# A two-layer decoder trunk: expert weights in units of 1024, 1024, 1024 and 512 columns instead of four of 896, with six low-half buffers

## The chip, the core and the metric

The kernel runs on one core of a Trainium2 chip. Its time is that of one execution on the device in microseconds (us); lower is better. TensorE (PE) does the matrix products, and its weight loads run beside them (PEld); VectorE (DVE) and ScalarE (ACT) do the elementwise work, GpSimd (POOL) a little of it; SyncE (SP) issues the DMAs that bring the weights from HBM.

## The reference, cut to what matters

256 tokens of width 1024 go through two layers of token mixers, cross attention and a feed-forward part. In the first layer the latter is dense, in the second it has 8 experts, of which each token uses 2. All is in float32. The expert part, on which the change acts:

```python
D_MODEL, D_FF, N_EXPERTS, TOP_K = 1024, 3584, 8, 2
def swiglu(h, w_gu, w_down):
    g, u = jnp.split(h @ w_gu, 2, axis=-1)
    return (jax.nn.silu(g) * u) @ w_down
def moe_ffn(h, router_w, w_gu, w_down):
    ...
    for e in range(N_EXPERTS):
        out = out + gate[..., e:e + 1] * swiglu(h, w_gu[e], w_down[e])
    return out
```

## The kernel before

**Three products for one.** Every float32 weight block is landed by a DMA in one of six slots of `raw`. ACT copies it, rounded to the fast float32r type, to `w_hi`; DVE subtracts that from `raw` and so gets the low half. The activations are split likewise. PE then does three float32r products for one exact one: high by high, high by low, low by high (`expert_products`), each with its own 128x128 stationary operand.

**A job.** For each expert, up to 128 of its tokens are gathered by products with a 0/1 matrix (`gather`, two halves), multiplied by the gate (g), up (u) and down (d) weights, and scattered back by another product (`scatter`). The inner width of 3584 is cut in `XUNITS` = 4 units of `XW` = 896 columns. `JOB`, made by `plan_job`, lists the 48 blocks of weights of a job as (g, u or d; unit; piece). A gate or up block has 256 rows of 896 columns (896 KB) and takes 2 k-tiles x 2 halves x 3 = 12 matmuls of 448 columns. A down block has 256 rows of 1024 columns (1 MB, 12 matmuls of 512 columns), the fourth of each unit 128 rows (6 matmuls). The order is g0 u0, g1 u1 d0, g2 u2 d1, g3 u3 d2, d3. A loop runs job after job; this input takes eight of them.

**The pipeline.** Each engine goes through the blocks in the same order with its own program. At block o PE does its products and then what `expert_after` puts behind it; ACT and DVE do `expert_work` of block o, if it has any, and then the weight work of a later block: ACT the high half of block o + `LEAD` (5), DVE the low half of block o + `LOW_LEAD` (3). The low halves go round in `EXPERT_LO` = 4 buffers, each borrowed from a tile of the mixers that is idle by then. SP issues the load of block b when the low half of block b - 6 is done, since that frees the slot. Semaphores tell how far each engine is: `raw_landed`, `hi_done`, `lo_done`, `block_used`.

**Between the blocks.** When a unit's gate and up sums are complete, ACT takes silu (`x_silu`), DVE multiplies (`x_hid`), PE transposes `x_hid` in seven 128x128 tiles (`turn_expert`) behind the last gate block of the next unit, and ACT and DVE split the result into high and low (`expert_turned`, in the text: the turn). For unit 3 this happens behind block (d,2,1). The gather for the next job stands behind (d,3,0) and (d,3,1) on PE; ACT and DVE split what it brings (`gathered`), DVE ahead of the low halves that follow in its program. The first job also holds the arithmetic of the routing on DVE (`routing_left`).

The function below is what PE does for a block, its waits ahead of the products; the rest of the touched code follows it.

Of the kernel before, what the change touches and what calls it, by code (L numbers as in the profile page):

```python
# [27 lines left out]
ALU = mybir.AluOpType  # L28
# [3 lines left out]
P = 128  # L32
# [21 lines left out]
EXPERT_LO = 4  # L54
LOW_LEAD = 3
UNIT = 512
XUNITS = 4
XW = 896
# [56 lines left out]
def plan_job():  # L115

    order = [(w, 0, i) for w in "gu" for i in range(4)]
    for v in range(1, XUNITS):
        order += [(w, v, i) for w in "gu" for i in range(4)] + [("d", v - 1, i) for i in range(4)]
    return order + [("d", XUNITS - 1, i) for i in range(4)]  # L120
# [20 lines left out]
def build(nc, x_in, mem_in, positions, norm_mix, w_in, attn_sink, w_branch, w_out, pool_w, pool_scale,  # L141
# [19 lines left out]
    assert len(DENSE) == FFN_BLOCKS and XUNITS * XW == F and 2 * XW <= 4 * UNIT  # L161
# [6 lines left out]
    with ctx:  # L168
# [27 lines left out]
        area_a = sb("area_a", [P, 2048])  # L196
        area_b = sb("area_b", [P, 2048])
# [6 lines left out]
        decay = sb("decay", [P, 4, T])  # L204
        pool_m0 = sb("pool_m0", [P, 4, 144])
        pool_m1 = sb("pool_m1", [P, 4, P])
        mask_a = sb("mask_a", [P, T])
        mask_c = sb("mask_c", [P, T])
# [64 lines left out]

        x_hid = area_a[:, 0:XW]
        x_silu = area_b[:, 0:XW]
        feed_t = view(area_b, 0, KD, T)
        expert_lo_bufs = [expert_lo0, expert_lo1, expert_lo2, expert_lo3]
# [121 lines left out]
        def expert_width(b):  # L399
            which, v, i = JOB[b[1] % len(JOB)]  # L400
            return 2 * XW if which != "d" else (D if i == 3 else 2 * D)
# [65 lines left out]
        def expert_source(e, o):  # L467
            which, v, i = JOB[o]
            if which == "d":
                rows = 2 * P if i < 3 else P  # L470
                return moe_w_down[0, bass.ds(e, 1), v * XW + i * 2 * P:v * XW + i * 2 * P + rows, :].rearrange(
                    "a (k p) n -> p (a k) n", p=P)
            col = v * XW + "gu".index(which) * F
            return moe_w_gu[0, bass.ds(e, 1), i * 2 * P:(i + 1) * 2 * P, col:col + XW].rearrange(
                "a (k p) n -> p (a k) n", p=P)
# [38 lines left out]
        def expert_hid_t(part, v):  # L514
            return stat1[:, part, 0:7, (v % 2) * P:(v % 2) * P + P]
# [14 lines left out]
        def _(sp):  # L530
# [8 lines left out]
            def load_expert(e, o, base, after_use=False):  # L539
# [6 lines left out]
                sp.dma_start(expert_raw(b).rearrange("p (k n) -> p k n", n=XW if JOB[o][0] != "d" else D),  # L546
# [166 lines left out]
        def _(act):  # L713
# [342 lines left out]
            def expert_work(j, o, first):  # L1056
# [3 lines left out]
                if which == "g" and i == 3:  # L1060
# [3 lines left out]
                    act.activation(x_silu[:, 0:448], bank[0][:, 0:448], ACT.Silu)  # L1064
                    act.activation(x_silu[:, 448:896], bank[1][:, 0:448], ACT.Silu).then_inc(ffn_silu.sem, 1)
# [11 lines left out]
                elif (which, v, i) == ("d", XUNITS - 1, 3):  # L1077
# [4 lines left out]
            def expert_turned(turn, v):  # L1082

                act.wait_ge(ffn_tr.sem, ffn_tr.at(turn, "tr"))
                act.activation(expert_hid_t(0, v)[:, 0:4, :], bank[4][:, :].rearrange("p (k n) -> p k n", k=4), ACT.Copy)
                act.activation(expert_hid_t(0, v)[:, 4:7, :], bank[5][:, 0:3 * P].rearrange("p (k n) -> p k n", k=3),  # L1086
                               ACT.Copy).then_inc(ffn_hi.sem, 1)
# [59 lines left out]
        def _(dve):  # L1147
# [495 lines left out]
            def expert_work(j, o, first):  # L1643
# [3 lines left out]
                if which == "u" and i == 3:  # L1647
# [4 lines left out]
                    dve.tensor_tensor(x_hid[:, 0:448], bank[2][:, 0:448], x_silu[:, 0:448], ALU.mult)  # L1652
                    dve.tensor_tensor(x_hid[:, 448:896], bank[3][:, 0:448], x_silu[:, 448:896], ALU.mult).then_inc(ffn_hid.sem, 1)
                elif which == "g" and i == 3 and v:
# [16 lines left out]
            def expert_turned(turn, v):  # L1671

                dve.wait_ge(ffn_hi.sem, ffn_hi.at(turn, "hi"))
                dve.tensor_tensor(expert_hid_t(1, v)[:, 0:4, :], bank[4][:, :].rearrange("p (k n) -> p k n", k=4),  # L1674
                                  f32_of(expert_hid_t(0, v)[:, 0:4, :]), ALU.subtract)
# [741 lines left out]
```

## Time and profile before

| | |
|---|---|
| Time, median of 3 runs | 2102.28 us (2102.07 to 2103.97) |
| The profiled execution | 2105.14 us, of which the span is 2103.4 us |
| Busy in the span | PE 2063.5, PEld 1771.3, DVE 1516.9, ACT 1273.9, POOL 56.0 us |
| HBM | 523.88 MB read, 250 GB/s over the span |
| TensorE clock granted | 0.993 of full speed on average |

The profiled execution is 2.86 us above the median of the runs; a difference worked out from its trace is set off from the median as it stands. A busy share sums over stages: a page of the profile gives it in 40 slices of 52.6 us, and the expert part fills the last 20.

### The profile page before, as it was taken

What the parts mean: (1) busy time and instruction counts of PE and PEld (TensorE: products, weight loads), DVE (VectorE), ACT (ScalarE), POOL (GpSimd) and SP (SyncE); (2) the same over time, 40 slices, a digit from 0 to 9 for tenths busy, and PEclk for the clock granted to TensorE, in tenths of its full rate; (3) what the DMA queues carried; (4) which work ended last, traced back from release to release, by engine and by line L of the source; (5) the groups of instructions that cost most, each with busy time, mean ns of one, the idle gap of its engine ahead of it and who ended that gap; (6) DMA issues with size and microseconds to landing.
All of it is one profiled execution on the core that took longest, in us unless ns stands there. A gap on an engine that the chain in (4) does not pass through costs nothing.

```text
span 2103.4 us, 26982 instructions
## 1 busy us (share of the span) xinstructions
PE 2063.5 (98%) x10103; PEld 1771.3 (84%) x10103; DVE 1516.9 (72%) x1498; ACT 1273.9 (61%) x1312; POOL 56.0 (3%) x134
## 2 busy tenths in 40 slices
PE   7999999999999999999989999999999999999997
PEld 6788888888888888888878888888888888888886
DVE  5776565555556776564379788888888888888897
ACT  6466545454344466545466766777666777767676
POOL 3300000000000300000000000000000000000000
PEclk9999999999999999999989999999999999999999
DMA  7444554455555444554469999899999999999994
GB/s 252 160 141 140 172 188 161 140 181 189 191 189 180 162 144 138 179 180 160 141 227 359 333 349 358 317 377 331 341 344 334 363 331 349 337 348 368 325 356 166
DMA packets 191708, 526.00 MB, mean 250 GB/s; under 512 B 10440, under 2 KB 17680, under 8 KB 191632
## 3 DMA queue, kind: packets, MB, share of 16 engines
q1 hardware_dynamic: 191632, 524.96, 70.4%
q8 instruction: 51, 0.84, 0.2%
q14 instruction: 25, 0.20, 0.0%
HBM read 523.88 MB, written 1.05 MB: 250 GB/s over the span
## 4 chain that ended last, share of the span: by engine, by line
PE 90%; DVE 5%; issue 2%; ACT 2%; SPq 1%; DMA 0%; POOL 0%; DVEq 0%; ACTq 0%
PE bank L1871 13%; PE bank L2269 13%; PE bank L1873 13%; PE bank L1872 13%; PE bank L2271 13%; PE bank L2270 13%; DVE expert_lo L1170 3%; PE bank L1904 2%; PE bank L2339 2%; PE bank L2349 1%; PE bank L2331 1%; PE bank L1940 1%; PE bank L1921 1%; PE bank L2019 1%; PE bank L2038 1%
## 5 line engine op out<-in xcount | busy, mean ns | idle before, releaser
L724 ACT ACTIVATE w_hi<-raw 128x1792 fp32r<-128x1792 f32 (+2 forms) x389 | 655.0, 1708 | 223.0 <-DMA raw<-in_moe_w_gu 179.2
L1170 DVE TENSOR_TENSOR expert_lo<-raw,w_hi 128x1792 fp32r<-128x1792 f32 (+2 forms) x387 | 758.4, 2017 | 0.9 <-ACT w_hi L724 0.7
L2269 PE MATMUL bank<-w_hi,stat 128*128 128x448 f32 (+1 forms) x1472 | 561.7, 382 | 8.0 <-DVE expert_lo L1170 7.9
L2271 PE MATMUL bank<-w_hi,stat 128*128 128x448 f32 (+1 forms) x1472 | 548.7, 373 | 0.0
L2270 PE MATMUL bank<-expert_lo,stat 128*128 128x448 f32 (+1 forms) x1472 | 548.5, 373 | 0.0
L1871 PE MATMUL bank<-w_hi,stat 128*128 128x512 f32 (+1 forms) x1296 | 512.1, 395 | 4.7 <-DVE low_in_place L1151 4.7
L1873 PE MATMUL bank<-w_hi,stat 128*128 128x512 f32 (+1 forms) x1296 | 504.4, 389 | 0.0
L1872 PE MATMUL bank<-low_in_place,stat 128*128 128x512 f32 (+1 forms) x1296 | 503.7, 389 | 0.0
L1151 DVE TENSOR_TENSOR low_in_place<-raw,w_hi 128x2048 fp32r<-128x2048 f32 (+1 forms) x162 | 368.8, 2281 | 185.5 <-ACT w_hi L718 185.1
L718 ACT ACTIVATE w_hi<-raw 128x2048 fp32r<-128x2048 f32 (+1 forms) x162 | 306.9, 1904 | 163.1 <-DMA raw<-in_dense_w_gu 57.2
L2269 PEld LDWEIGHTS bank<-w_hi,stat 128*128 128x128 f32 x1472 | 276.5, 188 | 51.5 <-DVE expert_lo L1170 15.5
L2270 PEld LDWEIGHTS bank<-expert_lo,stat 128*128 128x128 f32 x1472 | 276.8, 188 | 33.8 <-issue 3.3
L2271 PEld LDWEIGHTS bank<-w_hi,stat 128*128 128x128 f32 x1472 | 276.4, 188 | 33.4
L1871 PEld LDWEIGHTS bank<-w_hi,stat 128*128 128x128 f32 x1296 | 244.5, 189 | 55.4 <-issue 7.0
L1873 PEld LDWEIGHTS bank<-w_hi,stat 128*128 128x128 f32 x1296 | 244.3, 188 | 50.7
L1872 PEld LDWEIGHTS bank<-low_in_place,stat 128*128 128x128 f32 x1296 | 244.5, 189 | 47.7
L1674 DVE TENSOR_TENSOR stat<-bank,stat 128x512 fp32r<-128x512 f32 x32 | 22.1, 692 | 94.4 <-ACT stat L1086 94.4
L1093 ACT ACTIVATE stat<-bank,gains 128x128 fp32r<-128x128 f32 x72 | 20.5, 368 | 51.1 <-PE bank L2339 51.1
L1705 DVE SCALAR_TENSOR_TENSOR stat<-bank,gains,stat 128x128 fp32r<-128x128 f32 x72 | 20.3, 344 | 38.4 <-ACT stat L1093 38.4
L792 ACT ACTIVATE gate<-bank,rs_mix 128x512 f32<-128x512 f32 x16 | 11.0, 688 | 50.0 <-PE bank L1873 49.9
L2339 PEld LDWEIGHTS bank<-heads_t,tok 128*128 128x128 f32 x288 | 37.6, 205 | 2.3 <-issue 1.0
L1684 DVE TENSOR_TENSOR x<-x,bank 128x512 f32<-128x512 f32 x32 | 20.5, 684 | 25.9 <-PE bank L2349 25.9
(269 smaller groups left out, 1233.7 us busy)
## 6 DMA issues: line engine op xcount, KB each, us to landing
raw<-in_moe_w_gu SPq DMA_DIRECT2D x256, 896.0 KB, 7.0
raw<-in_moe_w_down SPq DMA_DIRECT2D x96, 1024.0 KB, 8.0
raw<-in_w_in SPq DMA_DIRECT2D x56, 1024.0 KB, 5.0
raw<-in_dense_w_gu SPq DMA_DIRECT2D x28, 1024.0 KB, 5.1
raw<-in_w_branch SPq DMA_DIRECT2D x16, 1024.0 KB, 5.0
raw<-in_w_xkv SPq DMA_DIRECT2D x16, 1024.0 KB, 5.1
raw<-in_moe_w_down SPq DMA_DIRECT2D x32, 512.0 KB, 7.8
raw<-in_dense_w_down SPq DMA_DIRECT2D x14, 1024.0 KB, 5.1
```

What stands on the lines that cost most here:

```text
L718: act.activation(w_hi[:, slot(b), :, 0:width], raw[:, slot(b), :, 0:width], ACT.Copy).then_inc(hi_done, 1)
L724: act.activation(expert_hi(b), expert_raw(b), ACT.Copy).then_inc(hi_done, 1)
L1151: dve.tensor_tensor(in_place_lo(b)[:, :, 0:width], raw[:, slot(b), :, 0:width], f32_of(w_hi[:, slot(b), :, 0:width]), ALU.subtract).then_i ...
L1170: dve.tensor_tensor(expert_low(b), expert_raw(b), f32_of(expert_hi(b)), ALU.subtract).then_inc(lo_done, 1)
L1871: pe.matmul(dst, x_hi, wh, start=start, stop=False)
L1872: pe.matmul(dst, x_hi, wl, start=False, stop=False)
L1873: return pe.matmul(dst, x_lo, wh, start=False, stop=stop)
L1904: ins = pe.transpose(b[:, i * P:(i + 1) * P], src, ident[:, :])
L2269: pe.matmul(dst[:, 0:n], x_hi, wh[:, at], start=start, stop=False)
L2270: pe.matmul(dst[:, 0:n], x_hi, wl[:, at], start=False, stop=False)
L2271: ins = pe.matmul(dst[:, 0:n], x_lo, wh[:, at], start=False, stop=stop)
L2339: ins = pe.matmul(bank[4 + i][:, k * P:(k + 1) * P], tok[:, t, kt * P:(kt + 1) * P], pick[:, t, :], start=(t == 0), stop=(t == NT - 1))
```

## The change

The inner width is cut in units of 1024, 1024, 1024 and 512 columns. Every block is now 1 MB (256 rows x 1024, or 512 rows x 512 for gate and up of unit 3), every block has 12 matmuls and every product of a block is 512 columns wide. A unit of 1024 has 4 pieces each of g, u and d, the unit of 512 has 2: 42 blocks a job. The matmuls of a job's blocks go from 384 of 448 columns and 168 of 512 to 504 of 512; the transposes stay 28. The low halves get six buffers, two more taken from tiles of the mixers (`area`, `shapes`), and are made one block further ahead (`LOW_LEAD` 4). The gather's first half stands behind (d,2,3), ahead of all of d3, with a wait for the split of unit 3's turned tiles (`ffn_lo`), whose banks it overwrites; its second half stands behind (d,3,0).

```diff
-EXPERT_LO = 4
-LOW_LEAD = 3
+EXPERT_LO = 6
+LOW_LEAD = 4
-XW = 896
+XW = [1024, 1024, 1024, 512]
...
+def pieces(v):
+    return XW[v] // 256
...
-        area_a = sb("area_a", [P, 2048])
-        area_b = sb("area_b", [P, 2048])
+        area, area_low = sb_shared("area", [P, 4096], "area_low", [P, 4096])
+        area_a, area_b = area[:, 0:2048], area[:, 2048:4096]
+        expert_lo4 = area_low[:, 1024:3072]
...
+        shapes, expert_lo5 = sb_shared("shapes", [P, 2112], "expert_lo5", [P, 2112])
...
-        expert_lo_bufs = [expert_lo0, expert_lo1, expert_lo2, expert_lo3]
+        expert_lo_bufs = [expert_lo0, expert_lo1, expert_lo3, expert_lo2, expert_lo4, expert_lo5]
...
+            rows = D // pieces(v)
+            return moe_w_gu[0, bass.ds(e, 1), i * rows:(i + 1) * rows, col:col + XW[v]].rearrange(
...
                 elif (which, v, i) == ("d", XUNITS - 1, 1):
                     gathered(j + 1, 1)
-                elif (which, v, i) == ("d", XUNITS - 1, 3):
                     act.wait_ge(block_used, used_at((job_base(j), o)))
                     act.activation(y_sb[:, 0:512], bank[6][:, :], ACT.Copy)
...
-                        at = slice((k * len(dsts) + h) * n, (k * len(dsts) + h) * n + n)
+                        at = slice((k * len(dsts) + h) * 512, (k * len(dsts) + h) * 512 + 512)
-                        pe.matmul(dst[:, 0:n], x_hi, wh[:, at], start=start, stop=False)
+                        pe.matmul(dst[:, :], x_hi, wh[:, at], start=start, stop=False)
...
-                    expert_products(b, [bank[two], bank[two + 1]], stat0, 2 * i, slice(0, P), 2, XW // 2, i == 0, i == 3)
+                    two, ktiles = 2 * "gu".index(which), KD // pieces(v)
+                    expert_products(b, [bank[two + h] for h in range(XW[v] // 512)], stat0, ktiles * i, slice(0, P),
+                                    ktiles, i == 0, last_piece(v, i))
...
                 elif (which, v, i) == ("d", XUNITS - 2, 1):
-                    turn_expert(turn + 1)
-                elif (which, v, i) == ("d", XUNITS - 1, 0):
+                    turn_expert(turn + 1, v + 1)
+                elif (which, v, i) == ("d", XUNITS - 2, 3):
+                    pe.wait_ge(ffn_lo.sem, ffn_lo.at(turn + 1, "lo"))
                     pe.wait_ge(pick_ready.sem, pick_ready.at(j + 1, "pick"))
                     gather(0)
-                elif (which, v, i) == ("d", XUNITS - 1, 1):
+                elif (which, v, i) == ("d", XUNITS - 1, 0):
                     gather(1)
```

DVE's program from the turn of unit 3 to the end of a job, before. The low buffer's number is the block's place modulo 4; the first row pair is the turn, the `stat0` rows are `gathered`.

```order
L1674 TENSOR_TENSOR stat1<-bank4,stat1 128x4x128
L1676 TENSOR_TENSOR stat1<-bank5,stat1 128x3x128
L1170 TENSOR_TENSOR expert_lo0<-raw,w_hi 128x2048
L1170 TENSOR_TENSOR expert_lo1<-raw,w_hi 128x2048
L1170 TENSOR_TENSOR expert_lo2<-raw,w_hi 128x2048
L1705 SCALAR_TENSOR_TENSOR stat0<-bank4,gains,stat0 128x128 x4
L1170 TENSOR_TENSOR expert_lo3<-raw,w_hi 128x1024
L1705 SCALAR_TENSOR_TENSOR stat0<-bank5,gains,stat0 128x128 x4
L1170 TENSOR_TENSOR expert_lo0<-raw,w_hi 128x1792
L1170 TENSOR_TENSOR expert_lo1<-raw,w_hi 128x1792
L1170 TENSOR_TENSOR expert_lo2<-raw,w_hi 128x1792
```

The row behind the turn is the low half of (d,3,0), and the first 128x1792 row, behind both `gathered`, that of (g,0,0) of the next job. The same stretch of DVE's program in the changed kernel, where `area_low` is the buffer of (d,3,0), `expert_lo5` that of (d,3,1) and `expert_lo0` that of the next (g,0,0):

```order
L1663 TENSOR_TENSOR area<-bank2,area 128x512
L1180 TENSOR_TENSOR expert_lo2<-raw,w_hi 128x2048
L1180 TENSOR_TENSOR area_low<-raw,w_hi 128x2048
L1688 TENSOR_TENSOR stat1<-bank4,stat1 128x4x128
L1180 TENSOR_TENSOR expert_lo5<-raw,w_hi 128x2048
L1180 TENSOR_TENSOR expert_lo0<-raw,w_hi 128x2048
L1180 TENSOR_TENSOR expert_lo1<-raw,w_hi 128x2048
L1718 SCALAR_TENSOR_TENSOR stat0<-bank4,gains,stat0 128x128 x4
L1180 TENSOR_TENSOR expert_lo3<-raw,w_hi 128x2048
L1718 SCALAR_TENSOR_TENSOR stat0<-bank5,gains,stat0 128x128 x4
L1180 TENSOR_TENSOR expert_lo2<-raw,w_hi 128x2048
```

The low half of (d,3,0) now stands ahead of the turn and that of the next (g,0,0) ahead of both `gathered`; the turn of unit 3 has one instruction for two. On PE, the first half of the gather stood before between the last product of (d,3,0) and the first of (d,3,1):

```order
L2269 MATMUL bank7<-w_hi,stat1 128x512
L2270 MATMUL bank7<-expert_lo0,stat1 128x512
L2271 MATMUL bank7<-w_hi,stat1 128x512
L2339 MATMUL bank4<-heads_t,tok 128x128 x8
L2269 MATMUL bank6<-w_hi,stat1 128x512
L2270 MATMUL bank6<-expert_lo1,stat1 128x512
```

Now it stands between the last product of (d,2,3), whose low buffer is `expert_lo2`, and the first of (d,3,0):

```order
L2282 MATMUL bank7<-w_hi,stat1 128x512
L2283 MATMUL bank7<-expert_lo2,stat1 128x512
L2284 MATMUL bank7<-w_hi,stat1 128x512
L2354 MATMUL bank4<-heads_t,tok 128x128 x8
L2282 MATMUL bank6<-w_hi,stat1 128x512
L2283 MATMUL bank6<-area_low,stat1 128x512
```

The gather moved up by one block. Between its second half and the next job's first block stands now (d,3,1), where (d,3,2) and the half block (d,3,3) stood before.

## Rows read from the trace of the kernel before

**Rows 1.** The page, by engine: busy us (share of the span) x instructions

```profile
PE 2063.5 (98%) x10103; PEld 1771.3 (84%) x10103; DVE 1516.9 (72%) x1498; ACT 1273.9 (61%) x1312; POOL 56.0 (3%) x134
```

**Rows 2.** The chain that ended last: start us, us, what

```profile
1183.34 1.78 PE bank L2339 x16
...
2077.70 1.78 PE bank L2339 x16
```

**Rows 3.** Groups by line and shape: shapes, count, busy us, mean ns, idle before

```profile
L1170 DVE TENSOR_TENSOR expert_lo<-raw,w_hi 128x1792 fp32r<-128x1792 f32 x259 | 508.8, 2017 | 0.9 <-ACT w_hi L724 0.7
...
L2269 PE MATMUL bank<-w_hi,stat 128*128 128x448 f32 x1024 | 383.4, 374 | 4.9 <-DVE expert_lo L1170 4.9
...
L1170 DVE TENSOR_TENSOR expert_lo<-raw,w_hi 128x2048 fp32r<-128x2048 f32 x96 | 215.9, 2282 | 0.0
L724 ACT ACTIVATE w_hi<-raw 128x2048 fp32r<-128x2048 f32 x96 | 181.7, 1928 | 37.0 <-DMA raw<-in_moe_w_down 36.9
...
L1170 DVE TENSOR_TENSOR expert_lo<-raw,w_hi 128x1024 fp32r<-128x1024 f32 x32 | 38.9, 1216 | 0.0
```

**Rows 4.** Waits on PE, from 1064 to 1112 us, then from there on

```profile
PE bank L2269 <- DVE expert_lo L1170: 2.7, 4, 1.0
...
PE bank L2269 <- DVE expert_lo L1170: 5.2, 16, 0.6
```

**Rows 5.** Timeline of PE, blocks without a wait: start us, us, instruction

```profile
1866.87 0.36 PE L2270 MATMUL bank<-expert_lo,stat 128*128 128x448 f32 x1
...
1876.39 0.40 PE L2269 MATMUL bank<-w_hi,stat 128*128 128x512 f32 x1
...
1881.62 0.39 PE L2271 MATMUL bank<-w_hi,stat 128*128 128x512 f32 x1
```

**Rows 6.** Timeline of PE at the end of a job

```profile
1813.96 0.93 PE L2331 MATMUL bank<-ident,area_a 128*128 128x128 f32 x7
...
1818.60 0.39 PE L2271 MATMUL bank<-w_hi,stat 128*128 128x512 f32 x1
1819.35 0.50 PE L2269 MATMUL bank<-w_hi,stat 128*128 128x512 f32 x1 [0.37 <-DVE expert_lo L1170]
1819.69 0.39 PE L2270 MATMUL bank<-expert_lo,stat 128*128 128x512 f32 x1
...
1832.38 0.39 PE L2271 MATMUL bank<-w_hi,stat 128*128 128x512 f32 x1
1833.00 0.47 PE L2269 MATMUL bank<-w_hi,stat 128*128 128x448 f32 x1 [0.23 <-DVE expert_lo L1170]
```

**Rows 7.** Timeline of DVE over the same stretch

```profile
1816.55 0.55 DVE L1676 TENSOR_TENSOR stat<-bank,stat 128x384 fp32r<-128x384 f32 x1
1817.02 6.68 DVE L1170 TENSOR_TENSOR expert_lo<-raw,w_hi 128x2048 fp32r<-128x2048 f32 x3
...
1829.89 1.13 DVE L1705 SCALAR_TENSOR_TENSOR stat<-bank,gains,stat 128x128 fp32r<-128x128 f32 x4 [2.26 <-ACT stat L1093]
1830.93 3.95 DVE L1170 TENSOR_TENSOR expert_lo<-raw,w_hi 128x1792 fp32r<-128x1792 f32 x2
```

**Rows 8.** Timeline of DVE at the routing and in the first job

```profile
1052.14 2.02 DVE L1170 TENSOR_TENSOR expert_lo<-raw,w_hi 128x1792 fp32r<-128x1792 f32 x1
...
1092.06 2.03 DVE L1170 TENSOR_TENSOR expert_lo<-raw,w_hi 128x1792 fp32r<-128x1792 f32 x1
...
1095.82 2.02 DVE L1170 TENSOR_TENSOR expert_lo<-raw,w_hi 128x1792 fp32r<-128x1792 f32 x1
```

**Rows 9.** DMA, 1370 to 1970 us: GB/s in 40 slices; queue: packets, MB, share; issues

```profile
GB/s 398 340 384 360 337 273 373 296 361 363 351 382 355 272 376 326 320 380 347 380 344 317 292 378 308 358 376 352 385 357 257 376 322 317 382 345 397 352 335 275
...
q1 hardware_dynamic: 58921, 206.98, 93.9%
...
raw<-in_moe_w_gu SPq DMA_DIRECT2D x150, 896.0 KB, 7.0
```

**Rows 10.** DMA in the dense part, 440 to 640 us, the queue's row

```profile
q1 hardware_dynamic: 19515, 37.59, 56.5%
```

More of the change, by code:

```diff
@@ L160, in build @@
     LAYER_BLOCKS = MIX_BLOCKS + FFN_BLOCKS
[L161 removed]
+    assert len(DENSE) == FFN_BLOCKS and sum(XW) == F and 2 * max(XW) <= 4 * UNIT
     assert len(JOB) % CYCLE == 0 and len(JOB) % EXPERT_LO == 0
@@ L1059, in expert_work @@
                 turn = j * XUNITS + v
-                if which == "g" and i == 3:
+                if which == "g" and last_piece(v, i):
                     act.wait_ge(block_used, used_at((job_base(j), o)))
@@ L1063, in expert_work @@
                         act.wait_ge(ffn_hid.sem, ffn_hid.at(turn - 1, "hid"))
-                    act.activation(x_silu[:, 0:448], bank[0][:, 0:448], ACT.Silu)
-                    act.activation(x_silu[:, 448:896], bank[1][:, 0:448], ACT.Silu).then_inc(ffn_silu.sem, 1)
+                    for h in range(XW[v] // 512):
+                        ins = act.activation(x_silu[:, h * 512:(h + 1) * 512], bank[h][:, :], ACT.Silu)
+                    ins.then_inc(ffn_silu.sem, 1)
                     if v:
@@ L1646, in expert_work @@
                 turn = j * XUNITS + v
-                if which == "u" and i == 3:
+                if which == "u" and last_piece(v, i):
                     dve.wait_ge(ffn_silu.sem, ffn_silu.at(turn, "silu"))
@@ L1651, in expert_work @@
                         dve.wait_ge(ffn_tr.sem, ffn_tr.at(turn - 1, "tr"))
[L1652 to L1654 removed]
+                    for h in range(XW[v] // 512):
+                        ins = dve.tensor_tensor(x_hid[:, h * 512:(h + 1) * 512], bank[2 + h][:, :],
+                                                x_silu[:, h * 512:(h + 1) * 512], ALU.mult)
+                    ins.then_inc(ffn_hid.sem, 1)
+                elif which == "g" and v and last_piece(v, i):
                     expert_turned(turn - 1, v - 1)
@@ L2259, in dense_unit_block, with expert_products @@
                     feed_rows(0, 1)
-            def expert_products(b, dsts, stationary, k0, cols, ktiles, n, first, last):
+            def expert_products(b, dsts, stationary, k0, cols, ktiles, first, last):
                 wh, wl = expert_hi(b), expert_low(b)
@@ L2307, in expert_after @@
                     scatter(j - 1, 1, 4)
-                elif which == "g" and i == 3 and v:
+                elif which == "g" and v and last_piece(v, i):
                     if v == 1 and not first:
```

63 lines of the change are left out of this document (31 added, 32 removed).

## The prediction, made before the changed kernel was run

> **What bounds the kernel now.** I read the page first. PE is busy 98% of the span [rows 1], at a clock that was granted to 0.993, so the question is not whether PE is fed but what spaces its instructions. The chain that ended last comes by the same gather once a job; over seven jobs (1183.34 to 2077.70) that is 894.36 us, 127.8 us a job [rows 2]. The waits by releaser say what PE lacks: in the first job it sits idle four times for 2.7 us, in the rest of the expert part 16 times for 5.2 us, each time for a low half from DVE [rows 4]. So PE's own spacing is the bound, and the waits are two small ones at the end of each job. The bound next to it is DMA: in 600 us of steady jobs its queue was busy 93.9% of the time [rows 9]. That is close enough to have to be priced. DVE is third; its low halves take, a job, 32 x 1.965 + 12 x 2.249 + 4 x 1.216 = 94.7 us of the 127.8, from busy time by count [rows 3].
>
> **Term 1, wider products.** The columns that pass through PE stay the same (384 x 448 = 336 x 512); 48 matmuls a job are saved, and with them what one costs beyond its columns. The timeline of PE gives the spacing. From 1866.87 to 1876.39 there are 47 steps of 448 columns, over three block borders: 202.6 ns each. From 1876.39 to 1881.62 there are 23 steps of 512: 227.4 ns [rows 5]. So a job's gate and up blocks take 384 x 0.2026 = 77.8 us now and 336 x 0.2274 = 76.4 us then: 1.4 us less, 11.2 over eight jobs. Two digits in the starts leave 0.2 us a job either way, 9.6 to 12.8. The border between blocks costs PE nothing (the 47 steps cross three), so fewer blocks save nothing more.
>
> The 64 more columns cost 24.8 ns; at that rate 448 columns are 174 ns, and 29 ns of each step are the price that 48 matmuls a job no longer pay. The Trainium skill ("TensorE: Matmul & The Clock Gate", section "Wait — 56ns, not 53.3ns?") gives columns by 2.4 GHz plus about 2.5 ns as the spacing; by it 48 matmuls less save 0.12 us a job, 1.0 in all, and the sum below would end 10 us higher. The rows are of this kernel's pairs of load and product, and I go by them.
>
> **Term 2, the wait at (d,3,0).** PE starts the last product of (d,2,3) at 1818.60 and the next at 1819.35, 0.52 us later than its spacing allows, and the one behind it comes 0.34 on, 0.11 late [rows 6]. On DVE the low half of (d,3,0) starts at 1817.02, right behind the turn of unit 3; it is the first of three in 6.68 us, so it takes about 2.25 and ends at 1819.3 [rows 7]. In the changed program this low half stands ahead of the turn, where DVE has time. What is late next is the turn's low part itself, for which PE now waits ahead of the gather, with the whole PE program queued behind it. It was done at 1817.10, PE's last product of (d,2,3) at 1818.8: 1.7 us to spare, and the turn of unit 3 now has one instruction for two on ACT and on DVE (0.55 less there). I take the wait as gone: 0.63 x 8 = 5.0 us.
>
> **Term 3, the wait at (g,0,0).** From 1832.38 to 1833.00 PE loses 0.39 us, and about 0.11 with the restart as above. DVE's low half starts at 1830.93, behind the `gathered` of 1829.89 [rows 6, 7]. Now it stands ahead of both. (g,0,0) then needs `gathered` of the first half: PE has (d,3,0), the second gather and (d,3,1) in between, 2 x 2.73 + 1.8 = 7.3 us, for a split of 1.13 us on DVE [rows 7] behind a like one on ACT. The second half is first used by (g,0,2), three blocks or 8.2 us behind its gather. Gone too: 0.50 x 7 = 3.5 us, since the last job has no next.
>
> **Term 4, the first job.** DVE does one step of the routing between each two of its low halves, which start 3.76 us apart (1092.06, 1095.82) [rows 8], while PE takes a block in 12 x 0.2026 = 2.43. PE waits four times, 2.7 us in idle time [rows 4]; with the restarts (0.63 lost for 0.37 shown above) that is about 3.8. Then a low half takes 2.25, so the distance is 4.0, a block 2.73; the loss per step stays 1.3. But one more block of low halves is ready, which is worth 2.7: 1.1 stays, 2.7 is won. Against it, the low half at 1052.14 stands ahead of the routing with nothing to hide it, and grows by 0.25 to 0.3. Net 2.4 us, between 0 (if DVE uses up the lead before) and 3.8.
>
> **Term 5, stray waits.** Of the 5.2 us, 8 x 0.37 + 7 x 0.23 = 4.6 are the two regular ones; 0.6 shown, some 1.0 lost, belong to one more. One block more of lead covers it: 1.0 (0 to 1).
>
> **What costs nothing.** DVE's low halves become 42 x 2.249 = 94.5 us a job, as now. Unit 3 is short, so less stands between things: the turn of unit 2 comes behind its last gate block, and only (u,3,0) and (u,3,1) are left ahead of (d,2,0). From the start of the transposes to DVE's end of the turn the trace shows 1813.96 to 1817.10, 3.1 us [rows 6, 7]; PE needs 0.9 for the transposes and 5.5 for the two blocks to get to (d,2,0). That is 3 us to spare, behind which the whole of d2 would stand. The copy of the job's output by ACT moves with the job's last block and keeps what follows it.
>
> **DMA, the cover that has to hold.** A job loads 42 x 1.0486 = 44.0 MB. The terms make it 127.65 - 1.4 - 0.63 - 0.50 = 125.1 us, so the mean rate goes from 345 to 352 GB/s. At a share of 93.9% the queue moved 206.98 MB in 600 us [rows 9]; a share of 100% at the same time per packet would be 367 GB/s, or 120.0 us a job. PE stays the bound by 5 us a job. While blocks follow each other without anything between, PE asks for 1.0486 MB in 2.73 us, 384 GB/s (377 now), and slices of 15 us show up to 398 [rows 9]. The loop of a slot also closes: 7.0 us to land for 896 KB [rows 9], so 8.0 for 1 MB, 1.9 and 2.25 for the halves [rows 3], 12.2 in all against six blocks or 16.4 us. The Trainium skill ("DMA: Bandwidth & Descriptors", section Specifications) gives about 358 GB/s as HBM's limit for a core. The slices above it disagree; and by it a job could not be shorter than 123.0 us, which still leaves PE the bound.
>
> **The sum.** 11.2 + 5.0 + 3.5 + 2.4 + 1.0 = 23.1 us off the profiled execution's 2105.14: 2082.0. The median of the runs is 2.86 lower, so off it: 2079.2, say 2079.5. With all terms at their low ends and the regular waits gone: 9.6 + 8.5 = 18.1, 2084.2; at their high ends 12.8 + 8.5 + 3.8 + 1.0 = 26.1, 2076.2. The likeliest case's own range is 2076 to 2085. A measurement of this kernel can tell a change from none at about 0.2%, 4.2 us.
>
> **The rivals.**
> - *Only the waits go.* The spacing of 512 was read on down blocks, whose stationary operand comes from another tile than that of gate and up. If the price of a matmul beyond its columns is not saved there, or the regular waits come back in another place, 5 to 11 us are missing: 2085 to 2092. By the page's rule on spacing, worked as rows (48 x 2.5 ns in place of 1.4 us a job), it would be 2089.7. Against it: the operand has the same shape and type in both. 0.14.
> - *DMA holds the pace.* If 93.9% is as full as the queue gets, a job stays at 127.65 us and only the first job's gain is left: 2098 to 2103. For it: ACT waits for transfers, 36.9 us for the down blocks alone [rows 3]. Against it: DVE hardly ever waits for them (0.7 us [rows 3]) and the slices at 398. 0.08.
> - *Slower: the new shapes of the gate and up transfers are dearer.* The dense part's rows of 2 KB moved 37.59 MB in 200 us at a share of 56.5% [rows 10]: 333 GB/s when full. If all transfers went like that, a job would take 132.2 us, 4.6 more than now: 2102 + 8 x 4.6 = 2139. It decides from where the full rate falls below 345. For it: 4 of 42 blocks do get rows of 2 KB. Against it: the other 38 have rows of 4 KB, longer than now; with 4 blocks at 333 and 38 at 367 the job needs 121.2 us. 0.05.
> - *More than forecast*, below 2076: the spacing at its better end and no wait left anywhere. 0.06.
> - *A new wait in the short unit*, some 1 us a job or more, in place of those removed: 0.05, about 2086 to 2095.
>
> The forecast keeps 0.62.
>
> **How the numbers follow.** 2079.5 is the likeliest case. From 2074 to 2094 lie the forecast, the first and the last rival and most of the fourth; left out are DMA's two, 0.13, and the rest of the fourth, 0.04. Faster by over 0.2% (below 2098): 0.88. Within: 0.06, nearly all DMA holding the pace. Slower: 0.06.
>
> **What would show it right or wrong.** The changed trace should show the spacing of gate and up products at 227.4 ns; 48 matmuls less per job; no idle time ahead of (d,3,0) and (g,0,0); gathers 125.1 us apart; DMA at 352 GB/s and a share near 95% or less; in the first job one or two waits of a microsecond together. If the gathers are 127 us apart with DVE waiting for ACT and ACT for DMA, the second rival is right. If the spacing in unit 3, where twelve products in a row go to one bank, or in the gate and up blocks is above 230 ns, term 1 fails.

## The result and the profile of the changed kernel

| | before | changed |
|---|---|---|
| Median | 2103.12 us (2102.07 to 2104.83, 4 runs) | 2076.7 us (2076.33 to 2077.05, 4 runs) |
| Ratio, 95% interval | | 0.9873 (0.9859 to 0.9886) |
| Profiled execution, its span | 2105.14, 2103.4 us | 2076.53, 2074.8 us |

The change makes the kernel 26.4 us faster, 1.3%. The page by engine, busy us (share) x instructions, answers to [rows 1], and its costliest groups to [rows 3]:

```profile
PE 2042.9 (98%) x9719; PEld 1699.7 (82%) x9719; DVE 1516.0 (73%) x1435; ACT 1258.4 (61%) x1248; POOL 56.0 (3%) x134
...
PE 96%; DVE 1%; ACT 1%; SPq 1%; issue 1%; DMA 0%; POOL 0%; DVEq 0%; ACTq 0%
...
L733 ACT ACTIVATE w_hi<-raw 128x2048 fp32r<-128x2048 f32 x341 | 636.2, 1921 | 105.7 <-PE bank L2284 65.0
...
L2282 PE MATMUL bank<-w_hi,stat 128*128 128x512 f32 x1344 | 534.5, 398 | 0.3 <-DVE stat L1718 0.3
```

The row of the page of before that goes with the last of these, both widths together:

```profile
L2269 PE MATMUL bank<-w_hi,stat 128*128 128x448 f32 (+1 forms) x1472 | 561.7, 382 | 8.0 <-DVE expert_lo L1170 7.9
```

384 matmuls are gone (8 x 48). The second line is the share of each engine in the chain that ended last: nearly all of it is PE (90% before, with 5% of DVE). The idle time ahead of L2282 is 0.3 us where L2269 had 8.0. ACT, which waited for transfers, now waits most for PE to give a `w_hi` buffer back (65.0 us): the engines ahead of PE run into its heels.

The chain of waits gives the pace, as in [rows 2]; L2354 is the gather, two rows a job:

```profile
1176.67 1.78 PE bank L2354 x16
1181.19 1.78 PE bank L2354 x16
...
2050.68 1.78 PE bank L2354 x16
2055.20 1.78 PE bank L2354 x16
```

From the first to the third row shown are seven jobs: 874.01 us, 124.86 each, against 127.8. In what follows a job is counted from its first gate product to the next job's. Before, six jobs behind the first took 127.45 to 128.35, 127.78 on average; the same jobs now take 124.86 each, all alike within 0.02. The waits of PE over the whole rest of the expert part, 1112 to 2076 us, in answer to [rows 4] (line and releaser: us, times, longest):

```profile
PE bank L2364 <- issue: 1.2, 1, 1.2
```

That is one pause in the tail, ahead of the last scatter; the 16 waits for low halves are gone. Around the gather, in answer to [rows 6], PE goes

```profile
1800.58 0.39 PE L2284 MATMUL bank<-w_hi,stat 128*128 128x512 f32 x1
1800.80 1.95 PE L2354 MATMUL bank<-heads_t,tok 128*128 128x128 f32 x16
1802.51 0.48 PE L2282 MATMUL bank<-w_hi,stat 128*128 128x512 f32 x1
1802.82 0.40 PE L2283 MATMUL bank<-area_low,stat 128*128 128x512 f32 x1
```

without a bracket, and DVE, in answer to [rows 7]:

```profile
1793.67 2.29 DVE L1180 TENSOR_TENSOR area_low<-raw,w_hi 128x2048 fp32r<-128x2048 f32 x1
1796.14 0.69 DVE L1688 TENSOR_TENSOR stat<-bank,stat 128x512 fp32r<-128x512 f32 x1 [0.19 <-ACT stat L1095]
...
1803.96 1.13 DVE L1718 SCALAR_TENSOR_TENSOR stat<-bank,gains,stat 128x128 fp32r<-128x128 f32 x4 [0.53 <-ACT stat L1103]
```

The low half of (d,3,0), `area_low`, is done at 1795.96; PE wants it at 1802.8. DVE's brackets, here 0.19 and 0.53, are its own spare time. DMA between 1370 and 1970 us, in answer to [rows 9]:

```profile
GB/s 411 335 403 362 338 310 321 346 402 326 400 357 365 321 317 332 380 354 379 378 369 341 318 287 376 408 340 382 346 361 319 330 330 395 335 400 365 348 318 324
...
q1 hardware_dynamic: 60098, 211.96, 94.6%
...
raw<-in_moe_w_gu SPq DMA_DIRECT2D x132, 1024.0 KB, 7.0
```

353 GB/s on average and landings in 7.0 us, as long as those of 896 KB before.

**Where the 28.6 us between the two spans lie.** The first expert product starts at 1065.80 before and at 1064.05 after; the first job takes 128.16 and 121.5; six more jobs give 6 x 2.92 = 17.5; from the start of the last job to the end it is 142.8 and 140.1. In all 1.75 + 6.66 + 17.5 + 2.7. The 1.75 is no work of the change. In windows (the granted TensorE clock is the third value from the end) the part ahead of the experts differs in one place, before and after:

```profile
60.00:80.00 20.00, 18.53 (x84) 14.88 (x83) 16.68 (x33) 6.00 (x7) 8.20 (x4) 0.91 0.47 156
```

```profile
60.00:80.00 20.00, 18.56 (x93) 14.97 (x93) 17.04 (x35) 6.18 (x8) 8.21 (x4) 1.00 0.48 158
```

In the profiled execution of the kernel before, the granted clock fell to 0.5, its 1.2 GHz level, for 3.4 us from 68.7 on, right behind a 1.47 us wait of PE for `gate`; after an equal wait in the other trace it did not. Up to there the starts of PE's matmuls in the two traces differ by 0.1 us at most, and from there to the experts by 1.7. That execution was 2.0 us above the median of the four runs, and so the medians differ by 26.4 and not by 28.6.

### The profile page after: what moved, and what is told of

It reads as the page before. It is cut to its first block, busy times and chain, and to the rows that moved or that the text cites. A ratio compares the mean times of both kernels' runs of the same rounds, so it can differ in the third digit from the quotient of the medians.

```text
span 2074.8 us, 26022 instructions
## 1 busy us (share of the span) xinstructions
PE 2042.9 (98%) x9719; PEld 1699.7 (82%) x9719; DVE 1516.0 (73%) x1435; ACT 1258.4 (61%) x1248; POOL 56.0 (3%) x134
## 4 chain that ended last, share of the span: by engine, by line
PE 96%; DVE 1%; ACT 1%; SPq 1%; issue 1%; DMA 0%; POOL 0%; DVEq 0%; ACTq 0%
PE bank L2282 15%; PE bank L2284 15%; PE bank L2283 15%; PE bank L1884 14%; PE bank L1886 13%; PE bank L1885 13%; PE bank L1917 2%; PE bank L2354 2%; PE bank L2364 1%; PE bank L2346 1%; PE bank L1953 1%; PE bank L1934 1%; PE bank L2032 1%; PE bank L2051 1%; SPq L541 1%
## 5 line engine op out<-in xcount | busy, mean ns | idle before, releaser
L733 ACT ACTIVATE w_hi<-raw 128x2048 fp32r<-128x2048 f32 x341 | 636.2, 1921 | 105.7 <-PE bank L2284 65.0
L1180 DVE TENSOR_TENSOR expert_lo<-raw,w_hi 128x2048 fp32r<-128x2048 f32 x284 | 637.3, 2287 | 0.2
L2282 PE MATMUL bank<-w_hi,stat 128*128 128x512 f32 x1344 | 534.5, 398 | 0.3 <-DVE stat L1718 0.3
L2284 PE MATMUL bank<-w_hi,stat 128*128 128x512 f32 x1344 | 524.2, 390 | 0.0
L1161 DVE TENSOR_TENSOR low_in_place<-raw,w_hi 128x2048 fp32r<-128x2048 f32 (+1 forms) x162 | 368.8, 2281 | 187.0 <-ACT w_hi L727 186.7
L2283 PE MATMUL bank<-expert_lo,stat 128*128 128x512 f32 x1120 | 436.2, 389 | 0.0
L2282 PEld LDWEIGHTS bank<-w_hi,stat 128*128 128x128 f32 x1344 | 252.5, 188 | 54.0 <-issue 3.4
L2284 PEld LDWEIGHTS bank<-w_hi,stat 128*128 128x128 f32 x1344 | 252.3, 188 | 53.3
L1884 PEld LDWEIGHTS bank<-w_hi,stat 128*128 128x128 f32 x1296 | 244.1, 188 | 55.3 <-issue 7.0
L1886 PEld LDWEIGHTS bank<-w_hi,stat 128*128 128x128 f32 x1296 | 243.9, 188 | 50.6
L2283 PEld LDWEIGHTS bank<-expert_lo,stat 128*128 128x128 f32 x1120 | 210.5, 188 | 45.4 <-issue 3.3
L1180 DVE TENSOR_TENSOR area_low<-raw,w_hi 128x2048 fp32r<-128x2048 f32 x56 | 128.2, 2289 | 8.1 <-ACT w_hi L733 8.1
L2283 PE MATMUL bank<-area_low,stat 128*128 128x512 f32 x224 | 87.2, 389 | 0.0
L2283 PEld LDWEIGHTS bank<-area_low,stat 128*128 128x128 f32 x224 | 42.1, 188 | 8.3
L1095 ACT ACTIVATE stat<-bank 128x512 fp32r<-128x512 f32 x56 | 31.0, 606 | 26.2 <-PE bank L2346 26.2
```

The costliest lines, as they stand in the source:

```text
L733: act.activation(expert_hi(b), expert_raw(b), ACT.Copy).then_inc(hi_done, 1)
L1161: dve.tensor_tensor(in_place_lo(b)[:, :, 0:width], raw[:, slot(b), :, 0:width], f32_of(w_hi[:, slot(b), :, 0:width]), ALU.subtract).then_i ...
L1180: dve.tensor_tensor(expert_low(b), expert_raw(b), f32_of(expert_hi(b)), ALU.subtract).then_inc(lo_done, 1)
L1884: pe.matmul(dst, x_hi, wh, start=start, stop=False)
L1886: return pe.matmul(dst, x_lo, wh, start=False, stop=stop)
L2282: pe.matmul(dst[:, :], x_hi, wh[:, at], start=start, stop=False)
```

## The experiments

**Theory**: the gain has three parts that add up. Wider products save PE some 1.4 to 1.7 us a job; the regular waits at (d,3,0) and (g,0,0) go because of the longer lead; the lead covers the routing in the first job. **Rival 1**: the regular waits have another cause that the new units or the gather's place take away by themselves, and the lead does nothing in a steady job. **Rival 2**: the products save less, and what looks like it is fewer waits.

**One part undone, or one done alone.** Three kernels start from the changed one. `a_width_only` keeps only the new units and the six buffers:

```diff
-LOW_LEAD = 4
+LOW_LEAD = 3
...
-                elif (which, v, i) == ("d", XUNITS - 2, 3):
-                    pe.wait_ge(ffn_lo.sem, ffn_lo.at(turn + 1, "lo"))
+                elif (which, v, i) == ("d", XUNITS - 1, 0):
...
-                elif (which, v, i) == ("d", XUNITS - 1, 0):
+                elif (which, v, i) == ("d", XUNITS - 1, 1):
```

`a_lead3` has the first hunk of this alone, `a_gather_late` the other two alone. Two start from the kernel before, with its four units of 896: `b_lead4` takes the six buffers, with the tiles that are lent for them, and the lead,

```diff
-EXPERT_LO = 4
-LOW_LEAD = 3
+EXPERT_LO = 6
+LOW_LEAD = 4
```

and `b_gather_up` the move of the gather alone (the hunks above in reverse).

Expected of `a_width_only`: 

> The changed kernel with the low halves three blocks ahead again and the gather behind (d,3,0) and (d,3,1) again, so that the new units and the six buffers are what is left of the change. Theory 1 (the prediction's own: the lead takes away the two regular waits): PE waits again at (d,3,0) and (g,0,0), 1.13 us a job, jobs 126.0 us apart, the waits of the first job are back with some 4 us and the stray ones with 1 to 2; about 2090. Theory 2 (the short last unit alone takes them away, since its turn is shorter and the next job's first low half then stands ahead of both splits of the gather): jobs stay within 0.2 us of 124.86, only the first job and stray waits cost, 4 to 6 us; about 2082.

Expected of `a_lead3`: 

> The changed kernel with the low halves three blocks ahead in place of four. Theory 1: the low half of (d,3,0) is behind the turn again, but the gather now stands ahead of that block and hides it; jobs at 124.9 us, first job and stray waits back, 4 to 6 us: 2081 to 2083. Theory 2 says the same number, and that a_width_only is no slower than this one. If the lead were worth the regular waits here too, it would be 2089 or more.

Expected of `a_gather_late`: 

> The changed kernel with the gather behind (d,3,0) and (d,3,1) again, four blocks of lead kept. Theories 1 and 2: no wait comes back, 2077, jobs at 124.9 us. Rival (the gather had to move because the unit of 512 leaves too few blocks behind it): PE waits at (g,0,0) or (g,0,2) for the split of the gathered rows, 0.5 to 2 us a job, 2081 to 2092.

Expected of `b_lead4`: 

> The kernel before, units of 896 and its own gather, with six low buffers and four blocks of lead. Theories 1 and 2: the waits at (d,3,0) and (g,0,0) go, jobs from 127.45 (the best of before) to 126.3 us; first job and stray waits go too, 4 and 2 us: 8.5 + 6 = 14 us less than before, about 2089. Rival (the waits move to something else in the same place, such as the split of the turn): less than 5 us gained, 2098 or more. If it gets below 2086, the spacing of the products is worth less than the 12 us I gave it.

Expected of `b_gather_up`: 

> The kernel before with the gather moved up by one block (behind (d,2,3) and (d,3,0), with the wait for the turn's low part ahead of it) and nothing else. Theory 2 (each part of the change removes the regular waits by itself, so their 8.5 us must not be counted once for each part): the waits at (d,3,0) and (g,0,0) go, jobs 126.5 us apart as in b_lead4, but the waits of the first job and the stray ones stay: 8 to 9 us below before. Theory 1 (only the lead takes them away): no more than 2 us below before.

| kernel | median us | ratio to before, 95% | first job | steady job |
|---|---|---|---|---|
| before | 2103.12 | | 128.16 | 127.45 to 128.35 |
| `b_gather_up` | 2094.16 | 0.9958 (0.9944 to 0.9973) | 127.70 | 126.48 |
| `b_lead4` | 2091.13 | 0.9935 (0.9918 to 0.9952) | 124.76 | 126.48 |
| `a_width_only` | 2081.97 | 0.9893 (0.9876 to 0.9909) | 123.86 | 124.86 |
| `a_lead3` | 2079.7 | 0.9881 (0.9864 to 0.9897) | 124.85 | 124.86 |
| `a_gather_late` | 2079.42 | 0.9885 (0.9868 to 0.9901) | 121.41 | 124.86 |
| changed | 2076.7 | 0.9873 (0.9859 to 0.9886) | 121.50 | 124.86 |

Each ratio is to the kernel before as measured together with that kernel, whose median was 2103.12 for the changed kernel, 2104.62 for `b_gather_up` and 2104.8 for the other four. The job lengths are from one trace each; the steady value is that of at least five of the six jobs, and the sixth is 0.14 us longer in `b_gather_up` and 0.05 in `a_width_only`.

The last column decides. There are two values for a steady job without waits: 126.48 with units of 896 and 124.86 with the new ones. Each part alone reaches the value of its units. The lead alone removes both regular waits, the gather's move alone removes both, and the new units alone do. Rival 1 holds in this form: the two waits had a margin so thin that any of the three edits covered it. The stray waits of the steady jobs go with them, in `b_gather_up` too, which has neither the lead nor the buffers (it keeps the 0.14 us). The six buffers were not run alone; before, DVE waited 0.9 us in all ahead of its low halves of 128x1792, 0.7 of it for ACT [rows 3], so hardly ever for a buffer. Rival 2 falls: with no wait on either side the new units are worth 126.48 - 124.86 = 1.62 us a job.

Beside the expectations: `a_width_only` came to 2081.97 where the second theory said about 2082 and the first about 2090, and `b_gather_up` to 10.5 us below its own before, where the second said 8 to 9 and the first at most 2. `a_lead3` came out 1.3 us under its range, `b_lead4` 2.1 us over its number (two waits of the first job stayed) and `a_gather_late` 2.4 us over, for a reason that neither theory had and that follows below.

The first job is where the lead still pays. PE's waits in `a_lead3` and, for comparison, in `b_lead4` (start, us, instruction, idle time before it):

```profile
1095.08 0.50 PE L2282 MATMUL bank<-w_hi,stat 128*128 128x512 f32 x1 [0.69 <-DVE expert_lo L1180]
1099.22 0.47 PE L2282 MATMUL bank<-w_hi,stat 128*128 128x512 f32 x1 [0.19 <-DVE expert_lo L1180]
1103.16 0.50 PE L2282 MATMUL bank<-w_hi,stat 128*128 128x512 f32 x1 [0.97 <-DVE expert_lo L1180]
1106.56 0.50 PE L2282 MATMUL bank<-w_hi,stat 128*128 128x512 f32 x1 [0.38 <-DVE expert_lo L1180]
```

```profile
1099.75 0.47 PE L2270 MATMUL bank<-w_hi,stat 128*128 128x448 f32 x1 [0.26 <-DVE expert_lo L1171]
1102.75 0.47 PE L2270 MATMUL bank<-w_hi,stat 128*128 128x448 f32 x1 [0.29 <-DVE expert_lo L1171]
```

With the new units, lead 3 leaves the four waits that the kernel before had, and 124.85 - 121.50 = 3.35 us is what lead 4 takes off. `a_width_only` has three such waits and a first job 1.0 us shorter than `a_lead3`, though PE's program is the same up to them; why one wait is missing was not followed up.

The gather's move shows only at the very end. The tail of `a_gather_late`'s chain, then of the changed kernel's:

```profile
2057.57 1.80 PE bank L2353 x16
2059.91 0.64 ACT stat L1103 x2
2061.09 0.61 DVE stat L1718 x2
2061.75 5.41 PE bank L2363 x8
```

```profile
2055.20 1.78 PE bank L2354 x16
...
2059.72 1.22 issue
2060.95 3.69 PE bank L2364 x8
```

At the old place the second gather stands next to the end, for a job that does not exist, and its split by ACT and DVE comes ahead of the last scatter: from the start of the last job to the end it takes 143.0 us and not 140.1. Of these 3.0 us, 1.25 are the later start of the last scatter. The other 1.7 are its length, 5.41 for 3.69: behind PE's wait of 2.4 us ahead of it the granted clock fell to 0.5, the 1.2 GHz level, from 2061.8 on for 3.4 us, and in the changed kernel it stayed at 1.0 there. `a_width_only` has the same wait, the same fall and the same 143.0. The last two kernels of the table differ by 2.7 us in the medians; steady jobs are alike. The kernel before had two more down pieces behind its second gather, which hid this. So with the new units alone the tail would have grown, and the move of the gather keeps it from that.

**The price of a matmul beyond its columns.** In the prediction this was 29 ns, a line through 448 and 512 columns. Four kernels take fewer columns in the block products of the changed one, so that a part of every product is left out (half, a quarter, an eighth, a sixteenth); loads, weights and everything else stay:

```diff
+                n = 384
...
-                        pe.matmul(dst[:, :], x_hi, wh[:, at], start=start, stop=False)
+                        pe.matmul(dst[:, 0:n], x_hi, wh[:, at], start=start, stop=False)
```

Expected with 384: 

> The changed kernel with 384 of the 512 columns in every product of a block; a quarter of each product is left out, all loads and splits stay. Linear theory (0.3875 ns a column and 29 ns a matmul, as the two widths of before give): spacing 178 ns. Floor theory (a matmul takes the longer of its columns and its weight load of 188 ns, and 14 ns more): 202 ns as with 448 columns. Page's rule (columns by 2.4 GHz and 2.5 ns): 162 ns. In each of these PE would need at most 112 us a job, so another engine sets the pace: DMA at 120.0 us a job by my estimate of 367 GB/s at a full share, 123.0 by the 358 GB/s of the page, below 115 if neither holds. VectorE has 110 us of work a job.

Expected with 256: 

> The same with 256 of the 512 columns; half of each product is left out. Linear theory: spacing 128 ns. Floor theory: 202 ns still. The job as in c_cols384 if DMA or VectorE is the bound there, since their work is the same.

Expected with 448: 

> 448 of the 512 columns in every product of a block (an eighth of each product is left out). With 256, 384 and 512 columns the spacing was 120.0, 173.6 and 227.2 ns, a line of 0.42 ns a column and about 13.5 ns beside it; at 448 that line gives 200.4 ns. If the 202.8 ns of the kernel before belongs to the width of 448, it shows up here again: 202.8 ns, and a job of 504 x 0.2028 + some 10.3 us of the rest = 112.5 us. If it belonged to the layout of the blocks before (rows of 896 columns in the weight operand), the spacing here is 200.4 ns and a job 111.3 us.

Expected with 480: 

> 480 of the 512 columns (a sixteenth of each product is left out). The line through 256, 384 and 512 gives 213.8 ns. If a width that is no multiple of 128 costs some 2.5 ns more in itself, it is 216.3 ns; if only 448 does, 213.8.

They ran once each and took 1955.76 (256), 1957.26 (384), 1985.79 (448) and 2035.44 us (480); what is read from them is the spacing in their traces. The first and the last start of 72 products in a row with 384, 448 and 480 columns, and with 512 in the changed kernel; between them are 71 steps:

```profile
1825.39 0.42 PE L2283 MATMUL bank<-w_hi,stat 128*128 128x384 f32 x1
...
1837.78 0.33 PE L2285 MATMUL bank<-w_hi,stat 128*128 128x384 f32 x1
```

```profile
1889.34 0.45 PE L2283 MATMUL bank<-w_hi,stat 128*128 128x448 f32 x1
...
1903.80 0.36 PE L2285 MATMUL bank<-w_hi,stat 128*128 128x448 f32 x1
```

```profile
1950.20 0.46 PE L2283 MATMUL bank<-w_hi,stat 128*128 128x480 f32 x1
...
1965.67 0.38 PE L2285 MATMUL bank<-w_hi,stat 128*128 128x480 f32 x1
```

```profile
1971.67 0.47 PE L2282 MATMUL bank<-w_hi,stat 128*128 128x512 f32 x1
...
1987.89 0.39 PE L2284 MATMUL bank<-w_hi,stat 128*128 128x512 f32 x1
```

The first step of a row holds some 0.08 us of the transposes ahead of it. Over the rows of the whole expert part without it and without waits the spacing is 173.6, 202.7, 216.7 and 227.1 ns; with 256 columns, where PE waits for DVE ahead of most blocks, it is about 120 ns within a block, here 20 steps in 2.40 us at a granted clock of 1.0:

```profile
1611.42 0.28 PE L2283 MATMUL bank<-w_hi,stat 128*128 128x256 f32 x1
...
1613.82 0.28 PE L2285 MATMUL bank<-w_hi,stat 128*128 128x256 f32 x1
```

None of the three spacings expected for 384 columns (178, 202 and 162 ns) came out. For 448 and 480 it is the theory in which the width itself costs more, 202.8 and 216.3 ns. Beside columns at 2.4 GHz (106.7, 160.0, 186.7, 200.0, 213.3 ns) there remain

| columns | 256 | 384 | 448 | 480 | 512 |
|---|---|---|---|---|---|
| ns beyond the columns | 13 | 13.6 | 16.0 | 16.7 | 13.8 |

There is a price of some 13.5 ns at every width, and the two widths that are no multiple of 128 cost some 2.5 to 3 ns more; whether it is this that they have in common, two widths do not show. It belongs to the width and not to the layout of the weights before: rows of 448 columns taken out of blocks of 512 show it too. So the 1.6 us a job have two sources: 48 matmuls less, 48 x 13.6 = 0.65 us, and 384 matmuls at an awkward width, 384 x 2.4 = 0.92 us; 1.57 together. A weight load is busy for 188 ns in every one of these kernels and yet products start 120 ns apart: it is no floor. The Trainium skill ("TensorE: Matmul & The Clock Gate", section "Wait — 56ns, not 53.3ns?") has 2.5 ns beyond the columns; these pairs of load and float32r product measure 13.5.

The same runs show what DMA can give. For 384 columns, 1300 to 1900 us: the queue, ACT's group and one of DVE's, then the window (behind its length the busy time of PE, PEld, DVE, ACT and POOL):

```profile
q1 hardware_dynamic: 68935, 244.36, 102.8%
```

```profile
L733 ACT ACTIVATE w_hi<-raw 128x2048 fp32r<-128x2048 f32 x234 | 446.7, 1925 | 105.0 <-DMA raw<-in_moe_w_gu 81.2 <-DMA raw<-in_moe_w_down 19.6 <-PE bank L2285 3.8
...
L1688 DVE TENSOR_TENSOR stat<-bank,stat 128x512 fp32r<-128x512 f32 x39 | 25.2, 683 | 9.1 <-ACT stat L1095 9.1
```

```profile
1300.00:1900.00 600.00, 564.12 (x3185) 531.07 (x3184) 590.95 (x400) 495.28 (x368) 0.00 (x0) 0.99 1.03 407
```

407 GB/s at a share of 102.8%, with ACT waiting for transfers and the steady jobs of both the 256 and the 384 column kernel at 107.7 to 109.1 us, 108.2 on average. The rate is the job's 44.04 MB by its length, so it is a rate that can be had and no proof that DMA is the bound there. DVE is busy 590.95 of the 600 us, 106.6 a job, and its idle time stands ahead of the turn's low part (9.1 us, 1.6 a job), none ahead of a low half: these two are the 108.2 us. The slices of 15 us stand at 409 or 410 GB/s in 30 of 40 and never above; at 410 the job's bytes would need 107.4. So DVE and DMA end within about 1% of each other, and which would hold the job alone no run here separates. With 448 columns the job is 112.89 us and with 480 it is 119.51, that is 504 x the spacing and 10.7 and 10.3 us, as it is 10.4 with 512: PE's again. The Trainium skill ("HBM Reference", section "Specifications (TRN2)") says that a core that streams alone measures well above the 358 GB/s of its share, about 425; 407 agrees with the first half of that, and no run here shows the 425.

**A version that might be faster still.** A job has two scatters of 4 matmuls, and behind each the next product starts late:

```profile
1836.09 1.88 PE L2364 MATMUL bank<-heads_t 128*128 128x512 f32 x4
1837.40 0.79 PE L2282 MATMUL bank<-w_hi,stat 128*128 128x512 f32 x1
1838.04 0.40 PE L2283 MATMUL bank<-expert_lo,stat 128*128 128x512 f32 x1
```

From 1837.40 to 1838.04 are 0.64 us where a step is 0.23: the second product comes 0.40 us late, against 0.08 behind a gather (1802.51 to 1802.82 above is 0.31). The experiment takes this for the price of a restart. `v_scatter_once` puts both scatters in one place, the second into banks 6 and 7:

```diff
-                elif not first and (which, v, i) == ("g", 1, 0):
-                    pe.wait_ge(scatter_added.sem, scatter_added.at(j - 1, "t0"))
-                    scatter(j - 1, 1, 4)
+                    scatter(j - 1, 1, 6)
```

The adding behind it on DVE moves likewise.

> The changed kernel with both parts of the scatter behind (u,0,0), the second into banks 6 and 7, in place of one there and one behind (g,1,0). PE is the bound with nothing waiting, so every restart of PE counts: behind a scatter the second product comes 0.40 us late, behind a gather or a transpose 0.08. One such restart less in seven jobs: jobs 124.4 to 124.5 us apart, 2.8 us less in all, about 2074. Rival (the 0.40 us are the price of each scatter matmul and move with it): jobs stay at 124.86.

2076.25 us (2075.72 to 2076.55), ratio 0.9867 (0.985 to 0.9883): the same as the changed kernel. Its steady jobs are 124.77, shorter by 0.09 us and not by 0.40, and its first job is 122.09, 0.59 longer, with a wait of PE for a low half (0.36 us at 1106.38); why was not followed up. The two cancel. PE's rows, and in the changed kernel the weight loads (PEld) ahead of the two products shown above:

```profile
1823.61 3.59 PE L2361 MATMUL bank<-heads_t 128*128 128x512 f32 x8
1826.64 0.79 PE L2281 MATMUL bank<-w_hi,stat 128*128 128x512 f32 x1
1827.27 0.40 PE L2282 MATMUL bank<-expert_lo,stat 128*128 128x512 f32 x1
```

```profile
1836.95 0.19 PEld L2364 LDWEIGHTS bank<-heads_t 128*128 128x128 f32 x1 [0.24 <-issue]
1837.38 0.19 PEld L2282 LDWEIGHTS bank<-w_hi,stat 128*128 128x128 f32 x1 [0.24 <-issue]
1837.81 0.19 PEld L2283 LDWEIGHTS bank<-expert_lo,stat 128*128 128x128 f32 x1 [0.24 <-issue]
```

There is no restart. Through a scatter one matmul follows the other by 0.43 us, as its loads do, and the product's row starts 0.03 us behind the last scatter matmul's (1837.38, 1837.40): the 0.40 are the rest of that matmul's own time. 1836.09 + 4 x 0.43 + one step of 0.23 is 1838.04, and 1823.61 + 8 x 0.43 + 0.23 is 1827.28. Eight in one place cost what twice four cost, the rival of the expectation. Behind a gather or the transposes it is the same with 0.11 us a matmul, of which 0.08 is left. Where the 0.09 us come from was not found.

## Why the prediction was right, and where its numbers were not

The forecast was 2079.5 us, its own range 2076 to 2085; 2076.7 is 2.8 us below the one and 0.7 inside the other. By its steps, in us, the measured side from job lengths:

| term | predicted | measured |
|---|---|---|
| 1, wider products | 11.2 (9.6 to 12.8) | 8 x 1.62 = 13.0 |
| 2 and 3, regular waits | 8.5 | 7 x 0.97 + about 0.5 = 7.3 |
| 4, first job | 2.4 (0 to 3.8) | 6.66 - 1.62 - 0.97 = 4.1 |
| 5, stray waits | 1.0 | 2.0 |
| sum | 23.1 | 26.4 |

0.97 is 127.45 - 126.48, the shortest job before against a job of its units without waits; 2.0 is what the six jobs before took above 6 x 127.45. To these 26.4 come the 1.75 of the clock and 0.5 in the tail that no term has. Three of the four rows came out above their own high ends (12.8, 3.8 and 1.0), one below its number, so the 26.4 are a little more than the 26.1 that the prediction had for all high ends at once. The last step, 2.86 off the profiled execution, was right: 1.7 of it is that execution's stretch at the lower clock. The gathers are 124.86 us apart where 125.1 was said. The mechanism holds; that the number stayed inside the range is in part luck, since three sizes of four were too small.

**Term 1**: right in kind, 0.22 us a job too small. The spacings read were right to half a ns (202.6 and 227.4 against 202.8 and 227.1 over thousands of steps). Times 384 and 336 these errors are 0.18 us a job, nearly all that is missing, and inside the 0.2 us that the prediction allowed for the two digits of the starts. What was wrong is the reading "29 ns of each step are the price that 48 matmuls a job no longer pay": the price is 13.5 ns, and the larger part of the gain is that 448 is a worse width than 512. Two points cannot tell a price per column from a price of a width. It did no harm, because both widths of the sum were the two that had been read. Had the units been cut to 480 columns, the line would have given 215.0 ns, and 216.7 is measured.

**Terms 2 and 3**: the waits went, as forecast, and their size was right to 15%. The cause given, that the low half now stands ahead of the turn, is enough but not needed, as the table of experiments shows. What the prediction called costless on the way (the turn of unit 3, the split of the gather, the wait on `ffn_lo`) was costless: there is no bracket on PE. The prediction has no term for the tail, where the old place of the gather would have cost 3.0 us with the new units.

**Term 4**: mis-sized. The step at fault is "one more block of low halves is ready, which is worth 2.7". That is a block of PE. A lead is worth a slot of DVE, since with it DVE has done one low half more behind the same number of routing steps, and a slot was worked out a line before: 4.0. The low halves of (u,1,1) and (u,1,2) in the changed kernel, DVE:

```profile
1096.04 2.29 DVE L1180 TENSOR_TENSOR expert_lo<-raw,w_hi 128x2048 fp32r<-128x2048 f32 x1
...
1100.08 2.29 DVE L1180 TENSOR_TENSOR expert_lo<-raw,w_hi 128x2048 fp32r<-128x2048 f32 x1
```

They are 4.04 apart and ready at 1098.3 and 1102.4; in `a_lead3` the same two blocks are ready 4.8 and 4.1 us later, by more than the 2.7 of a block of PE. One slot of DVE there is 4.0 us for the first and 3.4 for the second, without a routing step in it; the other 0.7 us were not followed up. So nothing of the waits stays where the prediction had 1.1 left. PE starts behind the nearest low half of the first job, that of (u,1,3), 0.14 us after it is ready: the lead was just enough, 3.35 us used and 0.14 left (`v_scatter_once` waits 0.36 us for this very block). The low half ahead of the routing grew from 2.02 to 2.29 us, as said; it cannot be told in the end time.

**Term 5**: the stray waits were 2.0 us and not 1.0. The prediction took them from what the two regular ones left of the idle time shown. One wait is shown, of 0.6 us at 1676.08, and makes its job 0.9 longer. Three more stand only ahead of weight loads, where PE's own rows have no bracket: 0.22 us at 1262.51, 0.42 at 1517.72 and 0.36 at 1547.72, each for a low half, in jobs that are 0.3 and 0.6 us longer.

**The rivals.** *Only the waits go*: out, the products save 1.62 us a job. *DMA holds the pace* and *dearer transfers*: out, 353 GB/s were drawn, and 407 are to be had with these same shapes. The estimate of 367 GB/s at full share was too low by at least 40: a busy share of 93.9% did not mean 6% of room but at least 18%. The bound by the HBM share, 123.0 us a job, was close to the 124.86 seen and had no part in it; jobs of 108 us show that. *A new wait in the short unit*: none. *More than forecast* came nearest: the spacing at its better end and no wait left anywhere is what happened, and yet the time stayed 0.7 us above that rival's 2076. *The gather's second half*, in term 3: "three blocks or 8.2 us behind its gather" held inside the run of jobs; what its old place does to the last job, 3.0 us with the clock, was seen only in `a_gather_late` and `a_width_only`.

## What to carry to other kernels

When an engine is busy 98% and every step depends on it, time its steps at the shapes of before and after, from long rows without a wait: the difference of two readings times the count is the forecast, and the price per instruction should not be split off from two points. A wait of a few tenths of a us per loop has little behind it; expect any edit that adds slack to remove it, do not count it twice, and test the edits one by one before giving one of them the credit. A lead on a producer is worth one step of that producer's own spacing where it is held up, not one of the consumer's; and work done for a next round that does not come belongs in the sum of the tail.

## What the runs showed of the hardware that was not expected

Products of 448 and 480 columns cost 16.0 and 16.7 ns beyond their columns at 2.4 GHz, those of 384 and 512 13.6 and 13.8. One core drew 407 GB/s from HBM over 600 us, at a queue share of 102.8%, so that shares of the queue near 94% still leave 15% of rate (353 to 407); no slice of 15 us in these windows was above 411. A matmul of the scatter (float32, 512 columns) follows the last by 0.43 us, one of the gather or the transposes (float32, 128 columns) by 0.11, a float32r product of 512 columns by 0.23; the row of the product behind a scatter starts 0.03 us after the last scatter matmul's. A wait of 1.47 us on PE at 67 us was followed by 3.4 us of the lower clock in one of the twelve traces and, at 1.3 to 1.5 us, by none in the other eleven; one of 2.4 us in the tail was followed by 3.4 us of it in both traces that have it.
